# Attention of the second layer with queries on partitions, rotary rows from doubled weight columns, and engine orders written out

## What is computed

```python
hk = rms_norm_2(x, kv_norm_g)
ckr = hk @ kv_w_down                                  # 1024 -> 256 + 32
c_kv = rms_norm_2(ckr[..., :KV_LORA], kv_latent_g)
k_rope = rope(ckr[..., KV_LORA:], cos, sin)           # one key part of 32 for all heads
kv = (c_kv @ kv_w_up).reshape(bsz, s_len, MLA_HEADS, QK_NOPE + V_HEAD)
k_nope, v_mla = kv[..., :QK_NOPE], kv[..., QK_NOPE:]
h = rms_norm_2(x, b_norm1_g[j])
proj = h @ b_w_in[j]                                  # 1024 -> 512 + 256
c_q = rms_norm_2(proj[..., :Q_LORA], b_q_norm_g[j])
q_mem = proj[..., Q_LORA:]
q = (c_q @ b_q_up[j]).reshape(bsz, s_len, MLA_HEADS, QK_NOPE + QK_ROPE)
q_rope = rope(q[..., QK_NOPE:], cos, sin)             # t1*cos - t2*sin, t2*cos + t1*sin
o = causal_mla_attention(q[..., :QK_NOPE], q_rope, k_nope, k_rope, v_mla)   # softmax, scale 96**-0.5
m = memory_attention(heads(q_mem, MEM_HEADS), mem_n, b_mem_kv[j])
x = x + jnp.concatenate([o, m], axis=-1) @ b_w_out[j]
```

## Time and profile before

| | us |
|---|---|
| median of three runs | 1172.21 (1171.92 to 1172.26) |
| the profiled execution | 1174.41 |
| its span, first to last instruction | 1172.6 |
| TensorE busy in it | 1088.0 |
| VectorE busy | 785.9 |
| ScalarE busy | 549.8 |
| GpSimd busy | 0.9 |

### The profile page before, as it was taken

How to read it: one execution, slowest core, us unless ns; L and a number is a source line. 1 busy time by engine, 2 the same in 40 slices (tenths; PEclk the granted TensorE clock), 3 DMA queues, 4 the chain that set the end, 5 groups by cost and what they waited for, 6 DMA issues and landing times.

```text
span 1172.6 us, 24104 instructions
## 1 busy us (share of the span) xinstructions
PE 1088.0 (93%) x10606; PEld 1024.4 (87%) x10606; DVE 785.9 (67%) x1249; ACT 549.8 (47%) x771; POOL 0.9 (0%) x7
## 2 busy tenths in 40 slices
PE   5999997999999999987889999999899889999997
PEld 4898887999899988876679999998886579999996
DVE  6797867877796668767456655666757856566553
ACT  5245363544575558543135444445454225444432
POOL 0000000000000000000000000000000000000000
PEclk9989999899999999999999999999999899999999
DMA  8867536145465462221015554465153004554461
GB/s 356 324 216 293 208 140 227 37 189 220 199 224 198 158 243 108 75 110 39 4 37 180 180 188 174 145 193 178 31 170 142 36 25 161 204 187 158 145 202 37
DMA packets 30377, 185.89 MB, mean 159 GB/s; under 512 B 3376, under 2 KB 4672, under 8 KB 12864
## 3 DMA queue, kind: packets, MB, share of 16 engines
q1 hardware_dynamic: 30272, 184.34, 43.7%
HBM read 183.28 MB, written 1.05 MB: 157 GB/s over the span
## 4 chain that ended last, share of the span: by engine, by line
PE 68%; DVE 18%; ACT 5%; DMA 5%; issue 4%; SPq 0%; DVEq 0%; ACTq 0%
PE banks L333 38%; PE banks L1230 15%; DVE wlo L293 5%; ACT whi L284 3%; DMA raw<-in_w_up 3%; PE banks L330 2%; PE banks L313 2%; DVE adac L500 2%; DVE adac L1434 1%; DMA con<-in_cons 1%; DVE S L500 1%; PE banks L1794 1%; DMA raw<-in_a_in 1%; DMA raw<-in_b_in 1%; PE banks L1801 1%
## 5 line engine op out<-in xcount | busy, mean ns | idle before, releaser
L293 DVE TENSOR_TENSOR wlo<-raw,whi 128x2048 fp32r<-128x2048 f32 (+4 forms) x174 | 340.4, 1956 | 218.0 <-ACT whi L284 217.9
L284 ACT ACTIVATE whi<-raw 128x2048 fp32r<-128x2048 f32 (+4 forms) x174 | 285.3, 1640 | 166.1 <-PE banks L1230 76.8
L333 PE MATMUL banks<-h_hi,whi 128*128 128x256 f32 (+1 forms) x1440 | 197.3, 290 | 9.3 <-ACT h_hi L2044 3.6
L333 PEld LDWEIGHTS banks<-h_hi,whi 128*128 128x128 f32 (+1 forms) x1440 | 183.8, 194 | 14.7 <-issue 5.2
L333 PE MATMUL banks<-h_hi,wlo 128*128 128x256 f32 (+1 forms) x1440 | 189.9, 284 | 0.1
L333 PE MATMUL banks<-h_lo,whi 128*128 128x256 f32 (+1 forms) x1440 | 188.1, 282 | 0.0
L333 PEld LDWEIGHTS banks<-h_hi,wlo 128*128 128x128 f32 (+1 forms) x1440 | 180.1, 192 | 2.1 <-issue 1.2
L333 PEld LDWEIGHTS banks<-h_lo,whi 128*128 128x128 f32 (+1 forms) x1440 | 176.3, 188 | 3.3 <-issue 2.6
L1256 ACT ACTIVATE u<-u 128x256 f32<-128x256 f32 x44 | 18.4, 418 | 130.2 <-DVE u L1310 130.2
L1230 PE MATMUL banks<-m_lo,whi 128*128 128x256 f32 x528 | 74.7, 280 | 0.0
L1230 PE MATMUL banks<-m_hi,wlo 128*128 128x256 f32 x528 | 74.6, 280 | 0.0
(11 more groups left out here) (477 smaller groups left out, 1445.4 us busy)
## 6 DMA issues: line engine op xcount, KB each, us to landing
raw<-in_ada SPq DMA_DIRECT2D x24, 1024.0 KB, 5.0
raw<-in_w_up SPq DMA_DIRECT2D x22, 1024.0 KB, 6.7
raw<-in_a_gu SPq DMA_DIRECT2D x22, 1024.0 KB, 4.8
raw<-in_b_gu SPq DMA_DIRECT2D x22, 1024.0 KB, 4.8
raw<-in_w_in SPq DMA_DIRECT2D x12, 1024.0 KB, 6.3
raw<-in_w_down SPq DMA_DIRECT2D x16, 704.0 KB, 4.2
raw<-in_a_in SPq DMA_DIRECT2D x11, 1024.0 KB, 5.7
raw<-in_a_down SPq DMA_DIRECT2D x16, 704.0 KB, 4.1
```

The lines of the kernel that those rows point to most:

```text
L284: act.activation(hi_s[k % NSPLIT][:, 0:w], raw[n % NRAW][:, 0:w], ACT.Copy).then_inc(*hi_made.tick(k))
L293: dve.tensor_tensor(lo_s[s][:, 0:w], raw[n % NRAW][:, 0:w], hi_s[s][:, 0:w].bitcast(F), SUB).then_inc(*lo_made.tick(k))
L333: i_ = pe.matmul(b[0:m, j * T:(j + 1) * T], a[:, kt * step + j * m:kt * step + j * m + m], x[:, kt, :], start=st, stop=sp)
```

## The change

The scores of a head have queries on the partitions. `pe_scores` takes the queries as the stationary side, so that a row holds one query's scores. VectorE takes negated row maxima from the bank, ScalarE writes exponentials with the maximum as bias and the row sums beside them, VectorE multiplies the weights by the reciprocals of the sums, TensorE transposes them, ScalarE copies them out, and `pe_values` multiplies. Spreading, the matmuls with ones, the wide reciprocals and the copies of the scores are gone. The scale of the scores is put into the query tables and into the memory queries.

For rotary chunks (kv_down 1 and q_up) the split writes 128 columns a block instead of 96: the 32 rotary columns, then the same with their halves exchanged. The product with one table (cosine, sine with its sign) is made as VectorE evacuates the chunk. For keys a matmul with a matrix `sel` adds the two halves, and ScalarE copies the result to all heads (`act_key_rope`); for queries the sum happens in the scores' matmul, now over 128 rows. There is one angle pass, done first. The constants, masks and buffers are fitted to it; weights in memory are as before. The latent and the query latent have buffers of their own. b_out's first chunk goes by input tiles, those of the memory heads first. The loops and slots are replaced by a written list of steps for each engine; `run(c, n)` advances chunk c by n of its parts (six a chunk, three for kv_down).

The diff, cut to what matters; first splits, then the steps of a head, the rotary parts and evacuations, then TensorE's list, the starts of ScalarE's and VectorE's lists and the end of VectorE's:

```diff
+        ROTARY = {("kv_down", 1)} | {("q_up", i) for i in range(6)}
+        TWICE = ((slice(0, 96), slice(0, 96)), (slice(96, 112), slice(80, 96)), (slice(112, 128), slice(64, 80)))
+
+        def by_96(b):
+            return b[:, 0:768].rearrange("p (k c) -> p k c", c=96)
+
+        def by_128(b):
+            return b[:, 0:1024].rearrange("p (k c) -> p k c", c=128)
...
+            if order[n] in ROTARY:
+                for to, of in TWICE:
+                    x = act.activation(by_128(hi_s[k % NSPLIT])[:, :, to], by_96(raw[n % NRAW])[:, :, of], ACT.Copy)
+                x.then_inc(*hi_made.tick(k))
+                return
...
+            if order[n] in ROTARY:
+                for to, of in TWICE:
+                    x = dve.tensor_tensor(by_128(lo_s[s])[:, :, to], by_96(raw[n % NRAW])[:, :, of],
+                                          by_128(hi_s[s])[:, :, to].bitcast(F), SUB)
+                x.then_inc(*lo_made.tick(k))
+                return
...
-        BY_TILE = {"w_out": [(n, kt) for kt in (0, 1, 2, 4, 5, 3, 6, 7) for n in range(3)]}
+        BY_TILE = {"w_out": [(n, kt) for kt in (0, 1, 2, 4, 5, 3, 6, 7) for n in range(3)],
+                   "b_out": [(n, kt) for kt in (6, 7, 0, 1, 2, 3, 4, 5) for n in range(3)]}
...
+        def pe_scores(pe, s):
+            key, S, cp, mx, sums, inv = slot(s)
+            a, b = rows_of(s)
+            if s >= 3:
+                pe.wait_ge(*at_a.at((("B", s - 3), "t")))
+            if s < 4:
+                pe.wait_ge(*b_v.at(("evac", 2)))
+                q, k = qk_mem(qmB, mkB, s)
+                pe.matmul(S[:, a], q[:, 0:P], k, start=True, stop=False)
+                x = pe.matmul(S[:, b], q[:, P:T], k, start=False, stop=True)
+            else:
+                h = s - 4
+                pe.wait_ge(*b_v.at(("evac", 14 + h // 2)))
+                pe.wait_ge(*b_a.at(("evac", 5 + h // 2)))
+                pe.wait_ge(*b_a.at("krope"))
+                pe.matmul(S[:, a], qc[:, h, 0:P], kc[:, h, 0:P], start=True, stop=False)
+                pe.matmul(S[:, b], qc[:, h, P:T], kc[:, h, :], start=False, stop=False)
+                x = pe.matmul(S[:, 0:384], M_ID, M_IL, start=False, stop=True)
+            x.then_inc(*at_p.tick((key, "s")))
+
+        def dve_maxima(dve, s):
+            key, S, cp, mx, sums, inv = slot(s)
+            dve.wait_ge(*at_p.at((key, "s")))
+            for j, w in enumerate(rows_of(s)):
+                x = dve.reduce_max(mx[:, j:j + 1], S[:, w], AX, negate=True)
+            x.then_inc(*at_v.tick((key, "max")))
+
+        def act_weights(act, s):
+            key, S, cp, mx, sums, inv = slot(s)
+            act.wait_ge(*at_v.at((key, "max")))
+            if s >= NS:
+                act.wait_ge(*at_p.at((("B", s - NS), "o")))
+            for j, w in enumerate(rows_of(s)):
+                x = act.activation(cp[:, w], S[:, w], ACT.Exp, bias=mx[:, j:j + 1], accum_out=sums[:, j:j + 1])
+            x.then_inc(*at_a.tick((key, "p")))
+
+        def dve_normed(dve, s):
+            key, S, cp, mx, sums, inv = slot(s)
+            dve.wait_ge(*at_a.at((key, "p")))
+            dve.reciprocal(inv, sums).then_inc(*at_v.tick((key, "inv")))
+            dve.wait_ge(*at_v.at((key, "inv")))
+            for j, w in enumerate(rows_of(s)):
+                x = dve.tensor_scalar(cp[:, w], cp[:, w], inv[:, j:j + 1], None, MUL)
+            x.then_inc(*at_v.tick((key, "norm")))
+
+        def pe_turn_q(pe, s):
+            key, S, cp, mx, sums, inv = slot(s)
+            pe.wait_ge(*at_v.at((key, "norm")))
+            if s < 4:
+                for ki in range(2):
+                    for qi in range(2):
+                        x = pe.transpose(S[:, ki * 256 + qi * P:ki * 256 + qi * P + P],
+                                         cp[:, qi * 256 + ki * P:qi * 256 + ki * P + P], C("ident"))
+            else:
+                for j in range(3):
+                    x = pe.transpose(S[:, j * P:j * P + P], cp[:, j * P:j * P + P], C("ident"))
+            x.then_inc(*at_p.tick((key, "t")))
+
+        def act_turned(act, s):
+            key, S, cp, mx, sums, inv = slot(s)
+            n = rows_of(s)[1].stop
+            act.wait_ge(*at_p.at((key, "t")))
+            act.activation(cp[:, 0:n], S[:, 0:n], ACT.Copy).then_inc(*at_a.tick((key, "t")))
+
+        def pe_values(pe, s):
+            key, S, cp, mx, sums, inv = slot(s)
+            o = o_bank(s)
+            pe.wait_ge(*at_a.at((key, "t")))
+            if s >= 4 and s % 2 == 0:
+                pe.wait_ge(*h_lo_made.at(("mixb", tile_b(s // 2 - 2))))
+            if s < 4:
+                v, rest = mvB[:, :, 64 * s:64 * s + 64], o
+            else:
+                h = s - 4
+                pe.wait_ge(*b_a.at(("evac", 11 + h // 4)))
+                v, rest = vc[:, :, 64 * h:64 * h + 64], o[:, P:T]
+            pe.matmul(o, v[:, 0, :], cp[:, 0:T], start=True, stop=False)
+            pe.matmul(rest, v[:, 1, :], cp[:, T:rows_of(s)[1].stop], start=False,
+                      stop=True).then_inc(*at_p.tick((key, "o")))
...
+        def tile_b(n):
+            return 6 + n if n < 2 else n - 2

         def act_mix_b(act, n):
-            f, src = mixed_b(n)
-            act.wait_ge(*at_v.at((("B", 2 * n + 1), "out")))
-            act.activation(h_hi[:, f, :], src, ACT.Copy).then_inc(*h_hi_made.tick(("mixb", f)))
+            f = tile_b(n)
+            act.wait_ge(*at_p.at((("B", 2 * n + 1), "o")))
+            act.wait_ge(*done_at("kv_down", 1))
+            act.activation(h_hi[:, f, :], bank[6 + n % 2][:, 0:T], ACT.Copy).then_inc(*h_hi_made.tick(("mixb", f)))

         def dve_mix_b(dve, n):
-            f, src = mixed_b(n)
+            f = tile_b(n)
             dve.wait_ge(*h_hi_made.at(("mixb", f)))
-            dve.tensor_tensor(h_lo[:, f, :], src, h_hi[:, f, :].bitcast(F), SUB).then_inc(*h_lo_made.tick(("mixb", f)))
+            dve.tensor_tensor(h_lo[:, f, :], bank[6 + n % 2][:, 0:T], h_hi[:, f, :].bitcast(F),
+                              SUB).then_inc(*h_lo_made.tick(("mixb", f)))
...
+        def act_sine(act):
+            act.wait_ge(*rope_v.at("clip"))
+            act.activation(ktab[:, :], posf[:, :], ACT.Sin).then_inc(*rope_a.tick("sin"))
+            act.preload_act_table_set(LN_EXP)
+
+        def dve_table(dve):
+            dve.wait_ge(*rope_a.at("sin"))
+            dve.tensor_scalar(qtab[ROPE, :], ktab[ROPE, :], QK_SCALE, None, MUL)
+            dve.tensor_scalar(qtab[0:64, :], ktab[0:64, :], 0.0, QK_SCALE, MUL, ADD).then_inc(*rope_v.tick("table"))
+
+        def pe_key_rope(pe):
+            pe.wait_ge(*b_v.at("kr"))
+            pe.wait_ge(*rs_a.at(("lat", "ln")))
+            pe.matmul(sbank[:, 0:T], C("sel")[ROPE, :], kr[ROPE, :], start=True, stop=True).then_inc(*b_p.tick("krope"))
+
+        def act_key_rope(act):
+            act.wait_ge(*b_p.at("krope"))
+            for n in range(2):
+                x = act.activation(kc[ROPE, 6 * n:6 * n + 6, :],
+                                   sbank[ROPE, 0:T].rearrange("p (a t) -> p a t", a=1).to_broadcast([64, 6, T]), ACT.Copy)
+            x.then_inc(*b_a.tick("krope"))
+
...
+            elif c == 2:
+                dve.scalar_tensor_tensor(out=qmB[:, :, :], in0=v2(b), scalar=0.125, in1=bc(rs_t[:, :], 2, T), op0=MUL,
+                                         op1=MUL).then_inc(*b_v.tick(("evac", c)))
+            elif name == "b_in":
+                dve.tensor_tensor(ct[:, 2 * i - 2:2 * i, :], v2(b), bc(rs_t[:, :], 2, T), MUL).then_inc(*b_v.tick(("evac", c)))
             else:
...
+                dve.wait_ge(*rope_v.at("table"))
+                dve.tensor_tensor(qc[:, 2 * i:2 * i + 2, :], v2(b), bc(qtab[:, :], 2, T), MUL).then_inc(*b_v.tick(("evac", c)))
...
+            run(0, 3)
+            mean()
+            run(1, 3)
+            run(2, 6)
+            mean_of("lat")
+            run(3, 1)
+            run(4, 1)
+            key_rope()
+            run(4, 2)
+            run(3, 5)
+            run(4, 3)
+            run(5, 6)
+            scores(0)
+            run(6, 6)
+            mean_of("qn")
+            run(7, 6)
+            run(8, 6)
+            scores(1)
+            scores(2)
+            run(9, 6)
+            turn(0)
+            run(10, 6)
+            run(11, 6)
+            run(12, 6)
+            values(0)
+            scores(3)
+            run(13, 6)
+            run(14, 6)
+            run(15, 6)
+            turn(3)
+            turn(1)
+            turn(2)
+            run(16, 3)
+            scores(5)
+            scores(6)
+            scores(4)
+            values(1)
+            run(16, 3)
+            values(2)
+            turn(5)
+            values(3)
+            turn(6)
+            run(18, 3)
+            turn(4)
+            scores(9)
+            scores(8)
+            values(4)
+            scores(7)
+            run(17, 6)
+            turn(9)
+            run(18, 3)
+            turn(7)
+            turn(8)
+            values(6)
+            values(5)
```

(63 more changed lines are left out.)

631 lines of the change are left out of this document (316 added, 315 removed).

## The result

The kernel after takes 1124.66 us (median of its runs, 1123.59 to 1130.4) beside 1172.07 us for the kernel before on the same chip (1168.88 to 1172.26). The ratio is 0.9612, with a 95% interval of 0.9575 to 0.9648. That is 47.4 us less, where 40 was forecast, and under the range's lower end of 1128 us. The profiled execution of the kernel after has a span of 1122.7 us, the one of before 1172.6.

A forecast was written before the change was run, and what follows sets the result against it. Bound by TensorE's own work and, from about 902 us, chains through VectorE. Work 23.6, waits 15.1 and clock 4.4 make 43.1 us; less 3.1 new, 40.0 off the 1172.2 median: 1132 us, range 1128 to 1141.

The forecast's parts named there:

- The work: Second layer's attention stage: spreading, sums by ones and query rotations leave TensorE, 23.6 us of work.
- 4.4 of clock: Two slow-clock stretches of the stage, 842.4 to 869.8 and 902.1 to 922.5 us, go with their gaps: 4.4 us.
- The change keeps scores, transposes and values: Per head on TensorE: these steps stay, scores with the same columns; a causal head's priced at 0.94, 0.24 and 0.70 us.
- All five waits: TensorE's waits in the attention stage for softmax (three), rotary sums and ScalarE's squares would go, 15.1 us.
- new waits: TensorE in the new stage, from replaying the engines' lists: 2.55 us, plus 0.6 for handovers of the memory heads.
- The start: Stage's beginning: VectorE's angles, behind the positions, come before kb_lo and the first evacuation; taken as 0.1 us of wait.
- The softmax on ScalarE: Per head: two exponentials at 0.8 us together plus 0.1 for each row sum, 1.0 us.
- Rival B: Softmax handovers: row sums cost their upper bound, 0.8 us a head more; 8 us slower, 1140; chance 0.12.
- the rule: Last triple of heads: transposes don't count for the clock gate, so TensorE could lose the clock; the sum kept 2.4 GHz.
- Rival C: New attention stage: the clock falls twice as before, so the 4.4 us stay; 1136.6; chance 0.09.
- Rival E: New stage's queues lock in their fixed order and heads go one after the other; 10 us slower, 1182; chance 0.03.
- the other stages have the same work: Everything outside the attention stage: same work, with next weights still landing more than one chunk ahead.

The follow-up runs named there:

- maxima_twice: The changed kernel with every head's row maxima taken twice on VectorE, the first into a scratch column; 1127.28 us, ratio 0.9606.
- Before_again: The kernel before, unchanged, run again for a second trace; 1173.16 us, ratio 1.0003.
- before_3: The kernel before, unchanged, traced once more for where the stage starts; 1173.15 us (one run).
- unpaired: The changed kernel with only TensorE's list altered, so other work stands between the steps of three adjacent pairs; 1132.29 us, ratio 0.9641.
- loops: The changed kernel's arithmetic with the written lists replaced by loops and slots like those of the kernel before; 1144.13 us, ratio 0.9747.

## Why the prediction was too cautious

**What bounds the kernel: right.** The gain is TensorE's work and TensorE's waits, in this one stage. VectorE's cover was real too (maxima_twice).

**The work: right in kind, 2.3 us short.** The stage's busy time fell by 30.3 us. The sum had 23.6 of work and 4.4 of clock, 28.0. The mean clock over the stage went from 0.95 to 0.98, not to 1.00: these two executions share a slow stretch at the start, a third one beside the two that the prediction counted. (Before_again and before_3 lack it, 130.3 and 130.4 us busy, and beside them the fall is 28.6.) What the term missed, as distances between starts in the two timelines:

- Pairs on separate halves of the array: scores(1) and (2) 1.03 us, two pairs of values 0.59 each, and the last three heads' values 1.45 in place of 2.10: 2.9 us that no line of the sum had. This is the step of the sum that failed. "The change keeps scores, transposes and values" was priced at the old rows, one head after another, and the order in the diff puts two side by side. The lower end allowed 1 us "for chunks that pack better" and nothing for this.
- A causal head's scores were not dearer with the 128-wide stationary side: 10.9 us for all twelve where twelve times 0.94 is 11.3: 0.3 us. The sum took them as equal, and that is nearly so.
- Against that the transposes: 0.25 to 0.48 a causal head, 4.7 for twelve, where I took 0.24, which was the start-to-start time up to the spreading matmul that now is gone: 1.8 us.
- And values that stand alone: 0.80 for 0.70 in five causal heads, 1.01 for 0.91 in the four memory heads: 0.9 us.

So the kept steps came to 0.5 us less than the sum had them (2.9 + 0.3 - 1.8 - 0.9), and the pairs were in great part eaten up by steps that cost more than their old rows. The rest of the 2.3 us can't be put down to one term: from the rows the dropped steps are 26.1 us (with the old values at the sum's prices) and not 23.6, since the sixth rotation (1.88 us) and the head behind it ran at the lower clock, and some 2.6 us came off chunks and means; the 4.4 of clock lie spread over both. The pairs' price itself doesn't hang on this sum: taken apart they cost 2.4 us of TensorE's time (unpaired). That the work came out within 2.3 us is in part luck: terms of 0.9 to 2.9 us that the sum did not have went both ways.

**The waits: right in mechanism, too dear.** All five waits of the earlier trace rows went, 15.1 us. Of the 3.15 us of new waits (2.55 and 0.6) less came: at the start 0.5 for 0.1, ahead of values(0) 0.4 for 0.6, none for chunk 18's low half, 0.6 before turn(13) for 0.75, none for turn(14) and turn(15), and 0.8 before turn(12) that the replay did not have. That is 2.3 us. The stage's idle time fell by 13.8 where the sum had 12.0; 15.1 - 2.3 = 12.8, and the last 1.0 are small gaps of the kernel before, two of them waits of 0.2. (The wait for X shrank by the 0.3 that were named, but lies ahead of the stage.) The start was the term most under-rated: VectorE does its angles first, behind the positions, and in the three executions of the kernel after these landed 4.5, 5.2 and 5.9 us after their issue, with a wait of 2.7, 3.3 and 4.0 behind, where the kernel before has 2.0 to 2.2. That is 0.5 to 2.0 us, for a term of 0.1.

**The softmax on ScalarE: right.** A causal head's weights in the kernel after, on ScalarE (timeline; the reading of the row sum is an instruction of its own):

```profile
898.15 0.36 ACT L2564 ACTIVATE hcp<-banks,hst 128x128 f32<-128x128 f32 x1
898.40 0.20 ACT L2564 ACTIVATION_READ_ACCUMULATOR hcp<-banks,hst 128x1 f32 x1
898.49 0.47 ACT L2564 ACTIVATE hcp<-banks,hst 128x256 f32<-128x256 f32 x1
898.85 0.21 ACT L2564 ACTIVATION_READ_ACCUMULATOR hcp<-banks,hst 128x1 f32 x1
898.94 0.38 ACT L2564 ACTIVATE hcp<-banks,hst 128x128 f32<-128x128 f32 x1
```

0.79 us from head to head (898.15 to 898.94), where I took 1.0. The row sum is 0.09 us from its start to the next one's (898.40 to 898.49), for an estimate of 0.1. Rival B, built on its upper bound, falls. The copies of the key are 1.4 us each, as bounded.

**The clock: right, and the rule did not show.** Rival C, two falls behind the start, did not come: from 823 us to the last value the clock is 1.00 in the kernel after. The longest run of transposes is here (timeline; the second fence is the stretch with the causal heads):

```profile
863.42 1.47 PE L2582 MATMUL banks<-con,hcp 128*128 128x128 f32 x12
864.65 1.18 PE L355 MATMUL banks<-c_hi,whi 128*128 128x256 f32 x8
```

```profile
863.40:903.70 40.30, 38.94 (x266) 31.45 (x264) 30.10 (x84) 26.92 (x79) 0.00 (x0) 1.00 0.42 157
```

Twelve transposes in a row, and the last triple's turns with a gap of 0.6 us, left the granted clock at 1.00, the upper level. The rule of the Trainium skill that transposes don't count for the gate ("TensorE: Matmul & The Clock Gate", Part 4: PE-mode transpose) is not refuted by this, since real work stood on both sides; it decided nothing here.

**The order as one rival only.** Rival E priced a locked order at 10 us slower than before. The loops kernel shows the new arithmetic in an unplanned order: 17.5 us slower than with the written one, and still 30 us faster than before. A lock as in rival E was built by no run.

**Outside the stage.** The sum gave the rest of the kernel nothing, beyond 0.3 to 0.4 us. The medians differ by 46.5 to 47.4, the stages by 42.2 in the mean of three executions each (149.0 and 106.8). Of the 4 to 5 us between, 0.8 to 1.0 stand behind the stage (212.2 to 212.4 us from its end to the span's in three executions before, 211.4 in three after) and the rest ahead of it, on TensorE's pace, as told above. So of the 7.4 us that the forecast missed against the medians, some 2 to 4 are the stage's (pairs and fewer waits), and the larger part lies outside. This is the second step that failed: "the other stages have the same work" was taken to mean the same time, and it was not. In the first result 3.4 us lie outside the stage (47.4 less 44.0); without them the time would have been 1128.1, just within the range. The mechanism of the stage was foreseen, the size of the whole was not, and why the other stages sped up is not known.

## What to carry to other kernels

When a change reorders an in-order engine, price the steps as they will stand side by side: two steps on different halves of TensorE's array cost about one of them when adjacent (0.81 and 1.07 us here), and both when other work stands between. A step's start-to-start time holds only for the neighbour it had, so a step whose successor is removed has to be priced anew. And ask of a wait that is closed which two next edges it had covered: closing 1.9 us at the start brought waits of 1.9 us back within two chunks.
